# Weaving the first of three token pieces of the closing products into the sample's key selection

## What is computed

```python
def layer_out(h, o_a, o_b, g_a, g_b, p_i, tail):
    merged = jax.nn.sigmoid(g_a) * (o_a @ w_br_a) + jax.nn.sigmoid(g_b) * (o_b @ w_br_b)
    h = h + rmsnorm(merged @ w_out, attn_post_g)
    gate, up = jnp.split(rmsnorm(h, ffn_pre_g) @ w_gate_up, 2, axis=-1)
    h = h + rmsnorm((jax.nn.silu(gate) * up) @ w_down, ffn_post_g)
    h = h + jax.nn.sigmoid(h @ w_ple_gate) * (p_i @ w_ple_proj)
    return h
# sample, branch A: score = sum_h w[t,h] relu(q_idx[t,h] . k_idx[s]) over 8192 + 4 keys, top 256 kept
```

## Time and profile before

| | us |
|---|---|
| median of 3 runs (3789.53 to 3810.14) | 3793.87 |
| the profiled execution | 3798.22 |
| its span, first to last instruction | 3796.6 |
| of this `sample_select`, 1092.2 to 1471.5 | 379.4 |
| of this `sample_attend`, 1471.5 to 3292.9 | 1821.4 |
| of this `tail`, 3292.9 to 3796.6 | 503.7 |
| PE busy, mean granted clock | 2962.3, 0.874 |

### The profile page before, as it was taken

The page is one execution under the profiler, slowest core; times in us unless marked ns, Lnnn a source line. Parts: engine busy times, 40 slices in busy tenths (PEclk is TensorE's granted clock), DMA queues, the critical chain, the costliest instruction groups (busy, mean ns, idle before and its releaser), DMA issues. The chain is left out here.

```text
span 3796.6 us, 66416 instructions
## 1 busy us (share of the span) xinstructions
PE 2962.3 (78%) x25067; PEld 1912.3 (50%) x25067; DVE 1525.1 (40%) x2849; ACT 572.2 (15%) x1203; POOL 587.0 (15%) x1089
## 2 busy tenths in 40 slices
PE   8999899369956001859888888886889887779998
PEld 4444366247756000535555555554556555446665
DVE  2222389667635883453333234335433200231102
ACT  1111200046634000010101011101101100010001
POOL 0000000000011000003333343324333442000000
PEclk9999699679968555979999889888999999889999
DMA  5322322310043004768998897988898864433333
GB/s 188 100 87 68 102 68 73 115 53 1 1 119 104 0 0 114 221 194 280 294 287 272 272 295 259 298 266 271 267 308 280 270 204 145 145 89 110 112 98 96
DMA packets 631343, 619.29 MB, mean 163 GB/s; under 512 B 64785, under 2 KB 503985, under 8 KB 630930
## 3 DMA queue, kind: packets, MB, share of 16 engines
q1 hardware_dynamic: 569106, 430.81, 37.5%
q0 software_dynamic: 61952, 184.62, 14.6%
HBM read 568.27 MB, written 46.98 MB: 162 GB/s over the span
## 5 line engine op out<-in xcount | busy, mean ns | idle before, releaser
L1223 PE MATMUL sa_t<-tw_z,tw_w 128*128 128x352 f32 x1664 | 553.5, 489 | 14.4 <-DMA tw_w<-w_out 10.6
L1478 POOL DMA_DIRECT2D sa_ring_v<-cache_b_kv x512 | 274.7, 537 | 1103.9 <-PE sa_o L1619 720.6
L1223 PEld LDWEIGHTS sa_t<-tw_z,tw_w 128*128 128x128 f32 x1664 | 327.9, 202 | 210.9 <-issue 68.2
L1712 DVE STREAM_TRANSPOSE sa_key_b<-sa_ring_k 128x2048 f32<-128x2048 f32 x128 | 294.0, 2304 | 173.4 <-DMA sa_ring_k<-cache_b_kv 101.2
L1223 PE MATMUL sa_t<-tw_x,tw_w 128*128 128x352 f32 x960 | 313.0, 485 | 51.2 <-DMA sa_new_sel<-new_bias 36.6
L213 PE MATMUL pr_acc<-pr_w,pr_u_t 128*128 128x512 f32 (+1 forms) x864 | 326.6, 539 | 0.0
L1479 POOL DMA_DIRECT2D sa_ring_va<-cache_a_kv x512 | 273.7, 535 | 54.5 <-issue 26.8
L1223 PEld LDWEIGHTS sa_t<-tw_x,tw_w 128*128 128x128 f32 x960 | 189.4, 201 | 163.8 <-issue 69.7
L1223 PE MATMUL ta_bank<-tp_z,tp_w 128*128 128x352 f32 x832 | 248.4, 462 | 5.6 <-DVE tp_z L1301 4.3
L213 PEld LDWEIGHTS pr_acc<-pr_w,pr_u_t 128*128 128x128 f32 x864 | 152.3, 190 | 167.9 <-issue 167.9
L1552 PE MATMUL sa_s<-sa_key_b,sa_q_pad 32*32 32x256 f32 x8192 | 191.5, 413 | 53.2 <-DVE sa_key_b L1712 48.3
(11 more groups left out here) (322 smaller groups left out, 3396.5 us busy)
## 6 DMA issues: line engine op xcount, KB each, us to landing
sa_ring_k<-cache_b_kv SPq DMA_DIRECT2D x512, 256.0 KB, 5.7
sa_ring_v<-cache_b_kv POOLq DMA_DIRECT2D x512, 256.0 KB, 6.2
tw_w<-w_gate_up SPq DMA_DIRECT2D x88, 512.0 KB, 8.1
sa_ring_ka<-cache_a_kv SPq DMA_DIRECT2D x512, 64.0 KB, 5.8
sa_ring_va<-cache_a_kv POOLq DMA_DIRECT2D x512, 64.0 KB, 5.9
tp_w<-w_gate_up SPq DMA_DIRECT2D x44, 512.0 KB, 3.8
tw_w<-w_down SPq DMA_DIRECT2D x32, 512.0 KB, 5.4
pr_w<-w_in SPq DMA_DIRECT2D x5, 2048.0 KB, 12.9
```

The source lines that it names most:

```text
L1223: ins = pe.matmul(bank[:, 0:PIECE], self.w[:, at % self.SLOTS, k - lo, :], moving[:, k, :], start=(k == 0), stop=(k == kc - 1))
L1478: pool.dma_start(ring_v[:, n % RING, :], rows_of(cache_b, page, 1)).then_inc(v_in[n // 4 % 2], 16)
L1712: nc.vector.transpose(key_b[:, at:at + 4].rearrange("p g n s -> p (g n s)"), ring_k[:, at:at + 4, :].rearrange("p g e -> p (g e)")).then_i ...
```

## The change

1. `Tail` now takes the first column and the width of its pieces, and stands ahead of `sample_select`. Widths stay at 352, so no matmul changes.
2. `sample_select` makes piece 0 (prefix `tx`, columns 0 to 351), `sample_attend` makes piece 1 alone, `tail` makes piece 2 as before.
3. In `sample_select` the loops over groups and counts are written out as a list of slots, with a planner of its own: a group of dot products weighs 2, a count 9, the ranking 27, and units are put behind a slot in proportion to that (2.14 us of units for a group, 9.6 us for a count, 28.9 us for the ranking). New scores are stored and loaded back in the middle of the first stage instead of behind it.
4. In `sample_attend` the budget of a step falls from 12.1 us to (483.9 - 60) / 75 = 5.65 us.
5. New `late`: on ACT and DVE, in both phases, the parts of unit g are held back and emitted where unit g+1 stands in the list. PE and SP walk over the list as it is.

```diff
-        rest = Tail(nc, a, ctx, "tw", ident, ones, t_bank, [0, 1])
+        rest = Tail(nc, a, ctx, "tw", ident, ones, t_bank, [FIRST], SECOND)
...
+        rest = Tail(nc, a, ctx, "tx", ident, ones, banks, [0], FIRST)
...
+        slots += [(kind, i) for i in range(COUNTS) for kind in ("count", "update")] + [("rank",), ("before",), ("bias",)]
+        weights = {"dots": BY_GROUP, "count": BY_COUNT, "rank": 3 * BY_COUNT}
+        share = sum(costs) / sum(weights.get(slot[0], 0.0) for slot in slots)
+        for slot in slots:
+            order.append(slot)
+            budget += share * weights.get(slot[0], 0.0)
+            while g < len(costs) and spent + costs[g] / 2 <= budget:
+                order.append(("rest", g))
+                spent += costs[g]
+                g += 1
...
+    def late(self, order):
+
+        out, held = [], []
+        for slot in order:
+            if slot[0] == "rest":
+                out += held
+                held = [slot]
+            else:
+                out.append(slot)
+        return out + held
...
-            for slot in order:
+            for slot in rest.late(order):
                 if slot[0] == "rest":
                     rest.scalar(act, slot[1])
...
-        rest = Tail(nc, a, ctx, "tp", ident, ones, banks, [2])
+        rest = Tail(nc, a, ctx, "tp", ident, ones, banks, [FIRST + SECOND], TOK - FIRST - SECOND)
```

More of the change, by code:

```diff
@@ L1090, with __init__ @@
     F_TILES = D_FF // P
-    def __init__(self, nc, a, ctx, name, ident, ones, banks, pieces):
+    def __init__(self, nc, a, ctx, name, ident, ones, banks, starts, width):
         ph = Phase(nc, ctx, name)
+        self.width, self.rows, self.left, pieces = width, width // P, width % P, starts
         self.nc, self.a, self.ident, self.ones, self.banks, self.pieces = nc, a, ident, ones, banks, pieces
@@ L1176, in sync @@
             sp.wait_ge(self.freed[g % 2], g // 2 + 1)
-            t0 = self.pieces[p] * PIECE
+            first, full, end = self.pieces[p], self.pieces[p] + self.rows * P, self.pieces[p] + self.width
             cols = slice(n * P, (n + 1) * P)
-            sp.dma_start(self.a["y"][t0:t0 + 2 * P, cols].rearrange("(j p) c -> p j c", p=P), self.y_row[:, n % 2, 0:2, :]).then_inc(self.stored[n % 2], 16)
-            sp.dma_start(self.a["y"][t0 + 2 * P:t0 + PIECE, cols], self.y_row[0:PIECE - 2 * P, n % 2, 2, :]).then_inc(self.stored[n % 2], 16)
+            sp.dma_start(self.a["y"][first:full, cols].rearrange("(j p) c -> p j c", p=P), self.y_row[:, n % 2, 0:self.rows, :]).then_inc(self.stored[n % 2], 16)
+            sp.dma_start(self.a["y"][full:end, cols], self.y_row[0:self.left, n % 2, self.rows, :]).then_inc(self.stored[n % 2], 16)
             if n == KC - 1 and p + 1 < len(self.pieces):
@@ L1194, in tensor @@
             pe.wait_ge(self.summed, 24 * p + {"n1": KC, "n2": 2 * KC, "n3": 3 * KC}[kind])
-            pe.matmul(bank[:, 0:PIECE], self.ones[:], self.sumsq[:], start=True, stop=True).then_inc(self.done, 1)
+            pe.matmul(bank[:, 0:self.width], self.ones[:], self.sumsq[:], start=True, stop=True).then_inc(self.done, 1)
             return
@@ L1198, in tensor @@
             pe.wait_ge(self.y_set, p * KC + n + 1)
-            for j in range(3):
-                rows = min(P, PIECE - j * P)
+            for j in range(self.rows + 1):
+                rows = min(P, self.width - j * P)
                 ins = pe.transpose(bank[0:rows, j * P:(j + 1) * P], self.y_t[:, n % 2, j * P:j * P + rows], self.ident[:])
@@ L1222, in tensor @@
                     pe.wait_ge(self.h_set, p * KC + k + 1)
-                ins = pe.matmul(bank[:, 0:PIECE], self.w[:, at % self.SLOTS, k - lo, :], moving[:, k, :], start=(k == 0), stop=(k == kc - 1))
+                ins = pe.matmul(bank[:, 0:self.width], self.w[:, at % self.SLOTS, k - lo, :], moving[:, k, :], start=(k == 0), stop=(k == kc - 1))
         ins.then_inc(self.done, 1)
@@ L1249, in scalar @@
                 act.wait_ge(self.freed[up % 2], up // 2 + 1)
-            nc.scalar.activation(self.sig[:, n % 2], bank[:, 0:PIECE], ACT.Sigmoid).then_inc(self.sig_set, 1)
+            nc.scalar.activation(self.sig[:, n % 2], bank[:, 0:self.width], ACT.Sigmoid).then_inc(self.sig_set, 1)
         if kind == "yg":
@@ L1254, in scalar @@
                 act.wait_ge(self.y_set, p * KC + n - 1)
[L1255 removed]
+            nc.scalar.activation(self.sig[:, n % 2], bank[:, 0:self.width], ACT.Sigmoid).then_inc(self.freed[g % 2], 1)
         if kind == "yt":
```

556 lines of the change are left out of this document (304 added, 252 removed).

## The result

| | before | after |
|---|---|---|
| median | 3791.7 us (3787.15 to 3810.14, 4 runs) | 3974.64 us (3971.12 to 3980.28, 4 runs) |
| span of the profiled execution | 3796.6 us | 3973.3 us |
| `sample_select` | 379.4 us | 762.8 us |
| of it: start to the first count (DVE's), counts 1 to 19, 19 to 30, the rest | 110.7, 131.2, 80.2, 57.3 | 263.6, 249.1, 135.2, 114.9 |
| `sample_attend` | 1821.4 us | 1609.7 us |

The change makes the kernel 4.6% slower: the ratio is 1.0463, with a 95% interval of 1.044 to 1.0487. I had forecast 3830 us and a range up to 3905, so the sign was right and the size was not. Of the 145 us between forecast and measurement, 120 lie in `sample_attend` and 19 in `sample_select`.

A forecast was written before the change was run, and what follows sets the result against it. PE idles in `sample_select`'s serial counting loop; in `sample_attend` PE and DMA are both nearly full, and DMA would become the bound. 3798.2 + 364 (`sample_select`) - 332 (`sample_attend`) = 3830 us, range 3745 to 3905.

The forecast's parts named there:

- `sample_attend`, steady steps: 54 steps of `sample_attend`: DMA becomes the bound at 312 GB/s, 23.9 to 19.2 us a step, -254 us.
- First nine steps: Start of `sample_attend`, only keys loaded: matmuls fall by 6.5 us a step, -48 us.
- the last ten: Last ten steps of `sample_attend`, only values: PE loses 65 us of work, POOL and landing replace it, -30 us.
- `late` at nothing: `sample_attend`: DVE's saved waits and the later starts of the norm chains both taken at no effect.
- `sample_select`, first stage: Before the counts: uncovered matmuls, exposed norm chains and first loads make PE's stage longer, +145 us.
- Counts 1 to 19: `sample_select` counting loop: threshold update waits for the `up` read-out, 12.6 us a count for 7.3, +101 us.
- Counts 20 to 30, the rest: `sample_select`: eight `dn` hide the loop, +52 us; last counts, ranking and last product with `n3` and rounds, +50 us.
- The +16 for restarts: `sample_select`: PE waits over 5 us eight times, each clock restart costing 2 us, +16 us.
- The best rate: Rival, `sample_attend`: transfers run at their best rate, 16.8 us a step, about 3700 us; chance 0.16.
- The two sides: Rival, both phases: steps near 18.6 us or `sample_select` 30 us less cancel the change, 3780 to 3812 us; chance 0.22.
- The low clock: Rival, counting loop: 2.6 us waits drop PE's clock, some 2 us x 19, +40 to +60, near 3880 us; chance 0.12.
- The units were hidden in the counts: Rival, `sample_select`: counts hide no units because the update waits for the `up`, 76 us more, 3905 us; chance 0.05.

The follow-up runs named there:

- e3: Changed kernel with the products (matmuls, weight loads, read-outs) left out of `sample_attend`: 3666.3 us, step 18.49 us.
- e7: Changed kernel without products in `sample_attend` and with the value ring holding two chunks instead of one: 3643.9 us, step 18.60 us.
- e8: As e7, with the key ring also holding two chunks and keys, branch A's included, asked for two chunks ahead: 3499.4 us, step 15.89 us.
- e6: Changed kernel with all matmuls kept in `sample_attend`, but weights loaded only four times and used again: 3920.8 us, step 20.35 us.
- e2: Changed kernel with `late` taken out in `sample_attend` only: 3970.0 us, step 21.13 us.
- e4: Changed kernel with four extra unread matmuls on PE ahead of each wait for counts 1 to 18 in `sample_select`: 3944.1 us.
- e5: Changed kernel with read-outs in `sample_select` held back two units instead of one: 3939.16 us, 1.0383 of before.
- e9: Changed kernel; `sample_attend`: key ring of two chunks, piece of 268 columns; `sample_select`: read-outs one unit late, two from the first count on: 3914.2 us.
- e13: Changed kernel with e9's `sample_select`, two pieces of 284 columns in `sample_attend`, rings unchanged, 136 columns in `tail`: 3767.3 us, 0.9929 of before.
- e14: As e9, with a 160-column piece, value ring of two chunks and branch A's keys asked for two chunks ahead: 3794.4 us, step 18.51 us.

## Why the prediction was wrong

Point by point, in its own steps.

**`sample_attend`, steady steps: this is the step that failed.** The term was -254 us, 19.2 us a step, and measured -154 us, 21.1 us. The bytes were right (321 MB / 54 = 5.95 MB a step, 6.0 forecast), and PE's work fell to 14.9 us a step, at a clock of 0.80, for the 13.3 forecast. The rate was wrong, 282 GB/s measured for 312: "I take 312 GB/s, between the 200 us and the 25 us row". Those rows were the best stretches of the old kernel; I read a rate that the loop had reached for 25 us as one that it would keep once PE was out of the way. The reason named in the same sentence, "Rings of one chunk don't let it run at its best all the time", was the real bound, and it deserved to be the sum itself: a half chunk of keys is asked for only when the one in its place has been turned, so a PE with less to do doesn't put more loads under way. The price at the unchanged rate, 21.3 us, stood in the text as the lower bound of the gain, and it was the nearest to the measurement. e3, e7 and e8 show it: without any product the step keeps 18.5 us with the keys asked for one chunk ahead, and falls to 15.9 with two. The piece then adds 2.6 us to the 18.5 (e3), of which 0.7 are its weights (e6); how the other 1.9 divide between PE's list and SyncE's is open.

**First nine steps and the last ten.** -48 forecast, -42 measured; -30 forecast, -13 measured. The last ten were mis-sized by 17 us, within the bounds given. The start of the phase gave 2 us. `late` at nothing: right (e2).

**`sample_select`, first stage.** +145 forecast, +153 measured. The chain ahead of `n2` was 17.8 us against 18.2, the first weights 13.5 against 9.

**Counts 1 to 19.** +101 forecast, +118 measured. The sequence was right: e4, with the clock kept up, gives 12.34 us for the forecast 12.6, and e5, with the `up` out of the update's way, 9.75 for 10.1. At 12.34 us the term is +91, for 18 intervals and not 19. What was wrong is "The 2.6 us waits of the counts I take at nothing": they cost 1.5 us each on average (e4), 27 us in 18 intervals, and 91 + 27 are the 118. The rival that named this had the mechanism and a chance of 0.12; with "some 2 us x 19" it was a little high. It was weighed with a stretch of the attention in which the clock stood at 0.91, a row that mixes many kinds of waits and says nothing of one that comes back every count.

**Counts 20 to 30, the rest.** +52 forecast, +55 measured; +50 and +58. The +16 for restarts can't be told apart from these stretches and the first stage. Without the counts' clock the phase would be at +356 for +364; in e4 it is at +352.

**The rivals.** The best rate did not come true, for the same reason as the forecast. The two sides did not cancel. The low clock came true. The units were hidden in the counts to the extent assumed. What I had no rival for is the case that decided, the transfers staying at their old rate; it appears only as the bound of -140 and in my list of what would prove me wrong ("steps above 21 us (then another loop than DMA is the bound, and the time is near 3900)"). With it and the low clock together, 3830 + 100 + 27, the forecast would have been 3957, within 18 us of the measurement.

**What the change does, then.** Its two sides are a piece taken out of the attention, worth 212 us, and put into the selection for 383. Its place in the selection costs 304 us if the evacuations stand where the loop doesn't wait for them (e9), still more than the 212 that the attention gives back. A woven column thus costs 0.86 us in the selection. It pays where the columns come out of `tail`, at 1.1 to 1.3 us a column (287.1, 379.1 and 505.7 us for 168, 252 and 352 columns). In e13, 216 columns come out of `tail` for -249 us and 136 out of the attention for -102, against the +304 of the selection.

## What to carry to other kernels

A stretch in which two resources look nearly full may be bound by neither: look at how much is asked for ahead, from which event the next request may go out, and how long the engine that issues it waits for that event, before you price a relief of either at a better rate. The rate to take is the measured one, unless the relief lengthens the queue of requests. When products are woven into a serial loop, count for each step of the loop which read-out its engine has in front of it, and price every recurring wait of the matrix engine with the clock that follows it.

## What the runs showed of the hardware that I had not expected

- In a loop in which PE is otherwise busy, 16 of 18 idle times of 2.25 to 2.6 us, one every 13.9 us, were followed by a stretch at a granted clock of 0.50 (changed kernel); behind the other two, of the same length, it stayed at 1.00. Four useless matmuls in the wait kept it at 1.00 in all 17 counts that followed the first, and gave back 1.5 us a count (e4).
- The same page loads moved 290 GB/s with one chunk asked for ahead and 338 GB/s with two (e3, e8), with the DMA share at 0.88 and 1.01. Doubling only the value ring gave 289 (e7).
- A DMA share of 0.87 to 0.89 stood beside 373 to 387 us in which SyncE waited before it issued a load (changed kernel and before, steady steps); at shares of 0.99 and 1.01 it waited 12 and 25 us (e14, e8).
